# Decay sums of a gated linear attention: table matmuls against differences of running sums

## The reference, cut to what matters

```python
la_gla = [split_heads(log_sigmoid(lr @ gla_gate_w[d] + gla_gate_b[d]) / GLA_GATE_NORM, GLA_HEADS) for d, lr in ...]

def chunked_recurrence(q, k, v, log_a, s0, chunk):
    ...
    bc = jnp.cumsum(log_a..., axis=3)
    b_last = bc[:, :, :, -1:, :]
    diff = bc[:, :, :, :, None, :] - bc[:, :, :, None, :, :]
    dec = jnp.exp(jnp.where(causal[:, :, None], diff, -jnp.inf))
    att = jnp.einsum('bhnid,bhnjd,bhnijd->bhnij', qc, kc, dec)
    o_intra = jnp.einsum('bhnij,bhnjv->bhniv', att, vc)
    q_in = qc * jnp.exp(bc)
    kv_chunk = jnp.einsum('bhnjd,bhnjv->bhndv', kc * jnp.exp(b_last - bc), vc)
    ...
```

## Time and profile before

| | us |
|---|---|
| median of 3 runs | 1762.56 (1758.4 to 1763.31) |
| the profiled execution | 1762.91 |
| its span in the trace | 1761.1 |
| PE busy | 1659.1 (94%) |
| DVE busy | 299.5 (17%) |
| ACT busy | 216.7 (12%) |
| POOL busy | 89.3 (5%) |

### The profile page before, as it was taken

The page is one execution under the profiler, slowest core; times in us unless marked ns, Lnnn a source line. Parts: engine busy times, 40 slices in busy tenths (PEclk is TensorE's granted clock), DMA queues, the critical chain, the costliest instruction groups (busy, mean ns, idle before and its releaser), DMA issues.

```text
span 1761.1 us, 42408 instructions
## 1 busy us (share of the span) xinstructions
PE 1659.1 (94%) x19946; PEld 1054.2 (60%) x19947; DVE 299.5 (17%) x703; ACT 216.7 (12%) x566; POOL 89.3 (5%) x148
## 2 busy tenths in 40 slices
PE   3999998999979999799999999999999999999994
PEld 0777546777758766565655555555556556555552
DVE  0244312000031462320010100100100101001003
ACT  1111222000021122100010100100100101001001
POOL 5021003000000220000000000000000000000000
PEclk7998898999989998799999999999999999999997
DMA  9546653444533371859989989999899899899970
GB/s 343 179 147 260 242 191 99 156 154 145 162 123 120 141 280 61 305 186 384 390 323 383 386 323 388 338 370 389 320 390 385 322 384 390 315 390 338 375 291 26
DMA packets 210447, 479.72 MB, mean 272 GB/s; under 512 B 8726, under 2 KB 54454, under 8 KB 203990
## 3 DMA queue, kind: packets, MB, share of 16 engines
q1 hardware_dynamic: 206876, 469.32, 72.8%
q0 software_dynamic: 3392, 7.63, 1.3%
HBM read 475.05 MB, written 1.87 MB: 271 GB/s over the span
## 4 chain that ended last, share of the span: by engine, by line
PE 92%; DVE 3%; ACT 2%; issue 2%; DMA 1%; POOL 0%; DVEq 0%; POOLq 0%; ACTq 0%
PE ps L1109 34%; PE ps L1129 17%; PE ps L1016 9%; PE ps L715 9%; PE ps L1024 4%; PE ps L1006 3%; PE ps L670 3%; PE ps L1079 2%; PE ps L1086 2%; PE ps L1116 1%; PE ps L900 1%; PE ps L746 1%; PE ps L747 1%; PE ps L702 1%; PE ps L764 1%
## 5 line engine op out<-in xcount | busy, mean ns | idle before, releaser
L1109 PE MATMUL ps<-arena,scratch 128*32 128x256 f32 x10752 | 605.4, 380 | 0.7 <-ACT scratch L1420 0.7
L1109 PEld LDWEIGHTS ps<-arena,scratch 128*32 128x32 f32 x10752 | 342.4, 110 | 240.1 <-issue 21.5
L1129 PE MATMUL ps<-arena,scratch 128*32 128x256 f32 x5376 | 300.5, 379 | 5.0 <-ACT scratch L1241 5.0
L1129 PEld LDWEIGHTS ps<-arena,scratch 128*32 128x32 f32 x5376 | 173.9, 110 | 120.9 <-ACT scratch L1241 6.9
L1817 DVE TENSOR_TENSOR scratch<-scratch,ps 128x128 f32<-128x128 f32 x168 | 48.4, 288 | 782.6 <-ACT scratch L1429 782.6
L715 PE MATMUL ps<-arena,hT 128*128 128x256 f32 (+1 forms) x704 | 156.8, 382 | 6.2 <-issue 6.2
L1016 PE MATMUL ps<-hT,arena 128*128 128x256 f32 x704 | 157.9, 383 | 3.0 <-issue 3.0
L1016 PEld LDWEIGHTS ps<-hT,arena 128*128 128x128 f32 x704 | 135.4, 192 | 30.8 <-issue 13.0
L715 PEld LDWEIGHTS ps<-arena,hT 128*128 128x128 f32 x704 | 133.0, 194 | 24.9 <-issue 7.3
L1429 ACT ACTIVATE scratch<-ps 128x128 f32<-128x128 f32 x168 | 46.7, 278 | 801.7 <-PE ps L1109 801.7
L557 POOL TENSOR_TENSOR stat<-stat,half_neg 128x1 f32<-128x1 f32 x10 | 8.3, 833 | 1409.2 <-DVE stat L1890 1025.2
(11 more groups left out here) (337 smaller groups left out, 917.6 us busy)
## 6 DMA issues: line engine op xcount, KB each, us to landing
arena<-in_moe_w_gate SPq DMA_DIRECT2D x112, 1024.0 KB, 8.4
arena<-in_moe_w_up SPq DMA_DIRECT2D x112, 1024.0 KB, 10.5
arena<-in_moe_w_down SPq DMA_DIRECT2D x112, 1024.0 KB, 13.9
arena<-in_w_mod SPq DMA_DIRECT2D x48, 1024.0 KB, 6.6
arena<-in_w_in SPq DMA_DIRECT2D x20, 1024.0 KB, 5.5
arena<-in_ffn_w_gate SPq DMA_DIRECT2D x11, 1024.0 KB, 5.4
arena<-in_ffn_w_up SPq DMA_DIRECT2D x11, 1024.0 KB, 7.9
arena<-in_ffn_w_down SPq DMA_DIRECT2D x11, 1024.0 KB
```

The source lines that it names most:

```text
L1109: ins = mm(ps[32 * g:32 * g + 32, 4 + i % 3, 0:256], e_h[:, kt, 32 * t:32 * t + 32], gate_up_pair(u, kt, g), start=(kt == 0), stop=(kt == ...
L1129: ins = mm(y_part(q, t), e_hidT[:, g, 32 * t:32 * t + 32], arena[:, at + QUARTER * q:at + QUARTER * q + QUARTER], start=(first and t % 2 = ...
```

## The change

The matrices `sum_qf`, `sum_qb`, `sum_kf` and `sum_kb` are gone from the constants: a partition's row in the second piece falls from 5476 to 1892 numbers. `gla_sums` now makes three running sums over all 128 tokens from the `scan` matrices that were there already: backward suffix, forward prefix, and backward suffix once more, 128 columns each, in one bank. For s = 0 two further matmuls of 128 columns serve the states; for s = 1 the running sums themselves serve. ACT copies the three running sums to SBUF (`run_sums`). DVE's new `gla_spans` then forms each of the 14 tables as a difference of two entries of the running sums by one `tensor_tensor`: one operand steps through the tokens, the other stays at the block's edge (a step of 0). ACT exponentiates the states' part meanwhile, and the 14 tables in place after a second wait. The banks of s = 1 are others than those of s = 0. The arena keeps its size but for 388 numbers a partition, because the experts use its place.

```diff
-          ("sin32", 16), ("iota", P), ("masks", LEVELS * P), ("sum_qf", LEVELS * P), ("sum_qb", LEVELS * P),
-          ("sum_kf", LEVELS * P), ("sum_kb", LEVELS * P)]
+          ("sin32", 16), ("iota", P), ("masks", LEVELS * P)]
...
-                for b, fwd, bwd in ((3, c("sum_qf"), c("sum_qb")), (5, c("sum_kf"), c("sum_kb"))):
-                    for lo, hi, bank in ((0, 4 * P, b), (4 * P, LEVELS * P, b + 1)):
-                        mm(ps[:, bank, 0:hi - lo], la_f, fwd[:, lo:hi], start=True, stop=False)
-                        mm(ps[:, bank, 0:hi - lo], la_b, bwd[:, lo:hi], start=False, stop=True)
-                for bank, la, d in ((4, la_f, 0), (6, la_b, 1)):
-                    left, right = (scan[:, d, :], la) if s == 0 else (la, scan[:, 2 + d, :])
-                    ins = mm(ps[:, bank, 3 * P:], left, right, start=True, stop=True)
+                for at, la, d in ((0, la_b, 1), (P, la_f, 0), (2 * P, la_b, 1)):
+                    ins = mm(ps[:, 3 + s, at:at + P], la, scan[:, 2 + d, :], start=True, stop=True)
+                if s == 0:
+                    for la, d in ((la_f, 0), (la_b, 1)):
+                        ins = mm(ps[:, 5, P * d:P * d + P], scan[:, d, :], la, start=True, stop=True)
                 ins.then_inc(sums_done, 1)
...
             def gla_decays(layer, s):
                 act.wait_ge(sums_done, NS * layer + s + 1)
-                a_.activation(g_x.rearrange("p l t -> p (l t)"), ps[:, 3:7, :].rearrange("p b n -> p (b n)"),
-                              ACT.Exp).then_inc(decays_ready, 1)
+                a_.copy(run_sums, ps[:, 3 + s, 0:3 * P]).then_inc(runs_kept, 1)
+                side = ps[:, 5, 0:2 * P] if s == 0 else ps[:, 4, P:3 * P]
+                a_.activation(g_x[:, 7::8, :], side.rearrange("p (d t) -> p d t", d=2), ACT.Exp)
+                act.wait_ge(spans_ready, NS * layer + s + 1)
+                spans = g_x.rearrange("p (k l) t -> p k l t", k=2)[:, :, 0:LEVELS, :]
+                a_.activation(spans, spans, ACT.Exp).then_inc(decays_ready, 1)
...
+        def run_view(at, block, step):
+            base = run_sums[:, at:at + 1]
+            return bass.AP(tensor=base.tensor, offset=base.offset, ap=[list(base.ap[0]), [block, P // block], *step])
...
+            def gla_spans(layer, s):
+                dve.wait_ge(runs_kept, NS * layer + s + 1)
+                for level in range(LEVELS):
+                    half = 64 >> level
+                    block = 2 * half
+                    for side, a0, ref0 in ((0, 0, half), (8, P, P + half - 1)):
+                        run = run_view(a0, block, [[P + half, 2], [1, half]])
+                        edge = run_view(ref0, block, [[P - 1 if side == 0 else P + 1, 2], [0, half]])
+                        out = g_x[:, side + level, :].rearrange("p (b h j) -> p b h j", h=2, j=half)
+                        if side == 0:
+                            ins = v.tensor_tensor(out, run, edge, ALU.subtract)
+                        else:
+                            ins = v.tensor_tensor(out, edge, run, ALU.subtract)
+                ins.then_inc(spans_ready, 1)
...
                 v.scalar_tensor_tensor(g_la, ps[:, 5:7, 0:256], 0.0, g_abs, ALU.min, ALU.subtract).then_inc(la_ready, 1)
+                gla_spans(layer, 0)
                 keep_projected(layer, 5)
...
                 o_finish(4 * layer, pj(0, "gv"), pj(0, "gog"))
+                gla_spans(layer, 1)
                 gla_decayed(layer, 1)
```

More of the change, by code:

```diff
@@ L48 @@
 N_CONST = _at
+N_FIXED = CCOL["masks"][0] + 2 * 2048
 PAGE = 2048
@@ L69, in constant_table @@
     put("ident", np.eye(P))
-    masks, sums = [], {"sum_qf": [], "sum_qb": [], "sum_kf": [], "sum_kb": []}
+    masks = []
     u, i = t[:, None], t[None, :]
@@ L76, in constant_table @@
         masks.append((block[:, None] == block[None, :]) & (second[:, None] != second[None, :]))
[L77 to L81, removed]
     put("masks", np.stack(masks, 1))
-    for name, a in sums.items():
-        put(name, np.stack(a, 1) / GLA_GATE_NORM)
     put("scan", np.stack([u > i, u < i, u <= i, u >= i], 1) / GLA_GATE_NORM)
@@ L151, in sem @@
             return ctx.enter_context(nc.semaphore(name))
-        arena = sb("arena", [P, 9 * PAGE + N_CONST + NS * IN_WIDTH + 2 * NS * D])
+        arena = sb("arena", [P, 9 * PAGE + N_FIXED + NS * IN_WIDTH + 2 * NS * D])
         at_area = SLOTS * PAGE
         at_const = 9 * PAGE
-        at_proj = at_const + N_CONST
+        at_proj = at_const + N_FIXED
         at_gates = at_proj + NS * IN_WIDTH
@@ L160, in hybrid_step @@
         area = arena[:, at_area:at_const]
-        const = arena[:, at_const:at_proj]
+        const = arena[:, at_const:at_const + N_CONST]
+        run_sums = arena[:, at_const + N_CONST:at_const + N_CONST + 3 * P]
         proj = arena[:, at_proj:at_gates].rearrange("p (s n) -> p s n", s=NS)
@@ L166, in hybrid_step @@
         moe_at = [PAGE * k for k in range(9)] + [at_tables, at_tables + PAGE, at_proj, at_proj + PAGE, at_gates]
-        assert len(moe_at) == MOE_SLOTS and 2 * PAGE <= N_CONST - CCOL["masks"][0] and 2 * PAGE + D <= NS * IN_WIDTH
+        assert len(moe_at) == MOE_SLOTS and 2 * PAGE <= N_FIXED - CCOL["masks"][0] and 2 * PAGE + D <= NS * IN_WIDTH
         final_g = arena[:, at_proj + 2 * PAGE:at_proj + 2 * PAGE + D]
@@ L318, in hybrid_step @@
                                                                   sem("lr_abs"), sem("lr_soft"), sem("la_ready"))
-        sums_done, decays_ready, decayed = sem("sums_done"), sem("decays_ready"), sem("decayed")
+        sums_done, runs_kept, spans_ready, decays_ready, decayed = sem("sums_done"), sem("runs_kept"), sem("spans_ready"), sem("decays_ready"), sem("decayed")
         g_att_done, g_att_kept = sem("g_att_done"), sem("g_att_kept")
```

## The result

The changed kernel takes 1735.84 us (median of four runs, 1735.46 to 1743.45) against 1762.3 before (1758.4 to 1763.31): a ratio of 0.9875, 95% interval 0.9841 to 0.9909. Run again later beside other kernels it took 1735.01 against 1761.53: 0.9851, interval 0.9826 to 0.9876. It is faster, by 3.2 us more than forecast, and inside the range. The profiled execution took 1735.82, its span is 1734.0, 27.1 less than before.

The account below looks back on a forecast made before the run. PE, busy 94% of the span, was taken to bound the kernel. From 1762.91 us, 22.34 for matmuls less 3.6 for waits plus 5.0 for the transfer gave 23.7 less: 1739, range 1733 to 1743 (chance 0.62).

Parts of the forecast that it names:

- Matmuls removed: PE's sums ahead of page 6: 5.36 us saved in stream 0, 5.81 in stream 1, 22.34 over two layers.
- The chain that grows: ACT and DVE work from sums to scores: 8.2 us in stream 0; PE waits 1.3 and 0.5, 3.6 in all.
- S: Length of DVE's 14 subtractions in each chain: 2.9 us, between 1.9 and 4.5.
- The transfer: Start: 1.84 MB fewer constants at 392 GB/s bring the last modulation page, and what follows, 5.0 us sooner.
- a gain at the start: If the clock stays high at the start, late pages' 1.89 us each and the transposes shrink, by up to some 3 us.
- No gain from the transfer: Rival, start: pages come no sooner because one queue alone moves less; 1744 us, chance 0.12.
- Linked rate: Rival, DVE's subtractions: each takes as long as if waiting for the one before, S = 4.5; 1746 us, chance 0.09.
- The clock falls in the waits: Rival, PE's four new waits: each brings some 4 us at the lower clock, about 2 us lost; 1747, chance 0.09.
- Slower, by short rows: Rival, DVE's subtractions: short inner rows of the operands cost extra; 1770 us at 15 ns a row, chance 0.03.
- c: Cost of each of the 508 inner rows in the 14 subtractions' operands; at 11.7 ns the whole gain is gone.

Follow-up runs that it names:

- linked: The changed kernel with each of DVE's 14 subtractions waiting for the one before; 1748.73 us median, ratio 0.9934 to the kernel before.
- halves: Changed kernel, query tables subtracted first, their Exp beside the key subtractions, states' multiplications ahead, page 5's copy behind, waits between multiplications removed; 1726.04 us median.
- Late_params: The changed kernel with the constants' second piece and all parameters issued only when seven modulation pages are used; 1728.1 us median, ratio 0.9823 to before.
- long_row: The changed kernel with 3200 unread zeros appended to each partition's row of the constants' second piece; 1747.74 us median, ratio 0.9925 to before.
- late_sums: The kernel before, with the sum matrices' 1.84 MB loaded by a transfer of their own behind the parameters; 1756.73 us median, ratio 0.9968.

## Why the prediction was right, and where its sizes were off

**Matmuls removed: right.** 5.33 us in stream 0 (93.34 to 94.47 against 96.66 to 103.12) for 5.36 forecast, and by the timeline 5.80 in stream 1 (120.50 to 121.27 against 127.78 to 134.35) for 5.81.

**The chain that grows: right, to 0.1 us.** 8.20 for 8.2, S 2.98 for 2.9, waits 1.30 and 0.45 for 1.3 and 0.5. That DVE, not ACT, is late in stream 1 held too: the subtractions follow `o_finish` at once (122.62 + 0.42 = 123.04), over 1 us after ACT's copy. The linked kernel shows that this chain is on the path, by adding to it, and halves by taking it away. The two mixer stretches together gave 18.5; the terms were 22.34 - 3.6 = 18.7.

**The transfer: the mechanism right, the term mis-sized.** It was 5.0, with the last page near 33.5; measured 3.3 to 3.5 (35.00). Over four executions with the short row and the parameters in place (both of the changed kernel, linked, halves), page 0 starts at 46.64 to 47.36, 3.0 to 3.7 us before the 50.37 of the one profile of before. I divided the missing bytes by the 392 GB/s of before. Once they were gone, something else stood beside the last pages. Both kernels' windows from 31 to 35 us, before and after:

```profile
31.00:35.00 4.00, 1.91 (x12) 0.13 (x15) 0.00 (x0) 0.00 (x0) 3.40 (x6) 0.50 1.01 404
```

```profile
31.00:35.00 4.00, 1.89 (x9) 0.11 (x10) 0.00 (x0) 0.00 (x0) 4.00 (x8) 0.50 1.05 338
```

The engines are as full, but move 338 GB/s instead of 404, and the pages still stand 3.6 apart. Late_params took away the parameters as well and brought them to 2.5 to 2.8. That the slower bytes are the projection's first pages, which SP had queued by then, is likely, because the rate was also low, 317 GB/s, from 38.5 to 50 us in the profile of before, but no run took them away alone.

**What was left out: the clock.** I priced a fall of the clock in the new waits (4 x 2 us, chance 0.09) and a gain at the start, which didn't come (the last pages still took 1.89 us each), but not that the clock of the untouched stretches moves by itself. This is the 5.3 us by which the profiled execution beat its sum, 27.1 against 21.8; the forecast's 23.7 was too high in one term by 1.7 and lacked this one. At equal clock the change is worth 22.5 us, close to the sum of the measured steps, 21.8. That the profiled execution came out within 3.4 us of the forecast's 23.7 is in part luck, since the two misses have opposite signs; with the clock of this stretch at its lowest, 0.81 as in linked, the same kernel would have been some 8 us slower.

**The rivals.** *No gain from the transfer* is refuted by long_row and late_sums. *Linked rate*: the subtractions overlapped; the linked kernel shows what it would have cost, 6.4 in waits and, in its profiled execution, 6.7 more at the lower clock behind them. *The clock falls in the waits*: not in the changed kernel, where 1.3 us left it at 1.00; it does behind the 2.9 and 2.1 us of linked. *Slower, by short rows*: the level with rows of one element cost 0.03 us an instruction; c would have had to be 11.7 ns, and 128 rows there cost 0.03 us, some 0.2 ns each. The Trainium skill's figure for hopping sources (Vector Engine (DVE) Microarchitecture Reference, "Measured stream behaviour on trn2"), an estimate of some 0.09 us by its 0.65 cycle an element, has the right sign; the trace shows a third of it, 0.03.

## What to carry to other kernels

When an engine that sets the end gives work to others, write down the whole new chain behind it, hand-overs included, and set it against the cover that is left: here it was known to 0.1 us before the run, and splitting it in halves so that it fell under the cover gave the rest of the gain. Moving transfers that nobody needs yet away from those that the first matmuls wait for was worth as much as shrinking them. And compare runs at equal granted clock, or stretches with the same instructions: a difference of medians (12 us for long_row) can be three or four times the effect (3.1 to 4.1). But look in the profile too, for an edit can lower the clock itself, as linked does, and then the equal clock hides half its price.

## What the runs showed of the hardware

**The mean granted clock goes with the time of a run.** With one core at work and nothing changed, the 30 runs of the kernel before go from 1749.91 us at 0.967 to 1765.16 at 0.956. In the two profiles of the changed kernel, whose spans differ by 3.0 us, the stretch behind the first mixers, with its many small matmuls and waits, differs by 3.2.

**POOL's small operations last until DVE's two-operand work is done.** The small rotary multiplications on POOL (16 columns) took 0.22 us each before, when DVE was idle, as this one in the trace of before:

```profile
99.02 0.22 POOL L587 TENSOR_TENSOR row<-arena 128x16 f32<-128x16 f32 x1
```

Where the change put them beside `gla_decayed`, they took up to 1.04 us:

```profile
99.93 0.99 POOL L585 TENSOR_TENSOR row<-arena 128x16 f32<-128x16 f32 x1
101.00 1.04 POOL L586 TENSOR_TENSOR row<-arena 128x16 f32<-128x16 f32 x1
102.12 0.25 POOL L587 TENSOR_TENSOR row<-arena 128x16 f32<-128x16 f32 x1
```

DVE's two multiplications of 896 columns lie at 99.75 and 100.87, 1.09 each, and the one of 128 columns at 102.00, 0.29. Each of the three POOL operations ends 0.08 us after the DVE operation beside it; DVE itself was not slowed. It cost nothing here, because nobody waited for POOL's result. In halves it did reach DVE: a POOL operation of 4 columns (L616) that took 1.04 us in the changed kernel took 3.12 beside the multiplications, and DVE waited 0.41 us for it, off PE's path.
